# Stick-breaking attention in a decoder block: VectorE's weight copies one slot later, the gather matmuls two slots later, the y copies two slots later

## What is computed

```python
def block(args):
    logits = jnp.einsum('bqhd,bkhd->bhqk', qi, k) * scale
    mask = key_pos[None, :] < q_pos[:, None]
    log_beta = jax.nn.log_sigmoid(logits)
    log_1m_beta = jnp.where(mask, jax.nn.log_sigmoid(-logits), 0.0)
    after = lax.cumsum(log_1m_beta, axis=3, reverse=True) - log_1m_beta
    w = jnp.where(mask, jnp.exp(log_beta + after), 0.0)
    return jnp.einsum('bhqk,bkhd->bqhd', w, v)
```

## Time and profile before

| | |
|---|---|
| median of 3 runs | 2943.34 us (2942.4 to 2946.0) |
| profiled execution, its own time | 2947.28 us |
| its span in the profile | 2944.7 us |
| mean granted TensorE clock | 0.970 of full speed |
| PE busy | 2750.3 us (93% of the span) |
| DVE, ACT, POOL busy | 1854.0, 1373.1, 924.1 us |
| the attention stage | from about 600 to 1096 us in the span |

### The profile page before, as it was taken

How to read it: one execution, slowest core, us unless ns; L and a number is a source line. 1 busy time by engine, 2 the same in 40 slices (tenths; PEclk the granted TensorE clock), 3 DMA queues, 4 the chain that set the end, 5 groups by cost and what they waited for, 6 DMA issues and landing times. The chain is left out here.

```text
span 2944.7 us, 43748 instructions
## 1 busy us (share of the span) xinstructions
PE 2750.3 (93%) x14835; PEld 2242.1 (76%) x14835; DVE 1854.0 (63%) x2853; ACT 1373.1 (47%) x2508; POOL 924.1 (31%) x839
## 2 busy tenths in 40 slices
PE   6999977879999989996999899999999999999998
PEld 5888864757777767885888688887888787878787
DVE  5343338958878876555667765656556748484853
ACT  4222224668878774323444455555554424242421
POOL 0011100746666652120000032333233334444442
PEclk9999988989999999997999999999999999999999
DMA  5433345282322204423222344334534465647554
GB/s 172 107 80 91 88 130 71 61 216 67 74 62 55 80 21 150 137 86 136 94 86 105 107 136 133 103 100 155 170 129 131 129 157 100 168 104 171 98 114 86
DMA packets 291144, 328.23 MB, mean 111 GB/s; under 512 B 113816, under 2 KB 220320, under 8 KB 290720
## 3 DMA queue, kind: packets, MB, share of 16 engines
q1 hardware_dynamic: 276704, 291.96, 33.2%
q0 software_dynamic: 13824, 33.56, 7.7%
q10 hardware_dynamic: 464, 0.79, 0.1%
HBM read 206.57 MB, written 126.88 MB: 113 GB/s over the span
## 5 line engine op out<-in xcount | busy, mean ns | idle before, releaser
L3252 PE MATMUL f_ps_bank<-f_big,h_wv 128*128 128x512 f32 x1280 | 503.0, 393 | 24.4 <-DVE f_big L3098 17.5
L3253 PE MATMUL f_ps_bank<-f_big,h_wv 128*128 128x512 f32 x1280 | 500.8, 391 | 0.0
L3254 PE MATMUL f_ps_bank<-f_big,h_wv 128*128 128x512 f32 x1280 | 500.7, 391 | 0.0
L736 POOL TENSOR_TENSOR a_w<-a_on,a_left 128x512 f32<-128x512 f32 (+3 forms) x320 | 304.3, 955 | 183.5 <-DVE a_left L784 168.8
L2995 ACT ACTIVATE h_wv<-h_w_sum 128x512 fp32r<-128x512 f32 x252 | 158.9, 631 | 347.0 <-PE f_ps_bank L3254 316.7
L2938 POOL TENSOR_TENSOR h_w_sum<-h_w_raw 128x512 f32<-128x512 f32 x63 | 90.2, 1432 | 731.1 <-DMA h_w_raw<-in_w_up 453.8
L3252 PEld LDWEIGHTS f_ps_bank<-f_big,h_wv 128*128 128x128 f32 x1280 | 241.9, 189 | 81.7 <-issue 26.3
L3254 PEld LDWEIGHTS f_ps_bank<-f_big,h_wv 128*128 128x128 f32 x1280 | 241.8, 189 | 50.9
L3253 PEld LDWEIGHTS f_ps_bank<-f_big,h_wv 128*128 128x128 f32 x1280 | 241.7, 189 | 49.5
L3094 DVE TENSOR_TENSOR h_wv<-h_w_raw,h_wv 128x512 fp32r<-128x512 f32 x189 | 175.1, 927 | 158.3 <-ACT h_wv L2995 154.2
L749 ACT ACTIVATE a_on<-a_ps_z 128x512 f32<-128x512 f32 (+3 forms) x320 | 170.9, 534 | 94.1 <-PE a_ps_z L842 53.0
(11 more groups left out here) (401 smaller groups left out, 6129.2 us busy)
## 6 DMA issues: line engine op xcount, KB each, us to landing
h_w_raw<-in_w_up SPq DMA_DIRECT2D x32, 1024.0 KB, 6.7
a<-h_xr SPq DMA_DIRECT2D x128, 256.0 KB, 3.4
h_w_raw<-a SPq DMA_DIRECT2D x32, 1024.0 KB, 5.2
h_raw<-in_w_down SPq DMA_DIRECT2D x32, 512.0 KB, 6.6
out<-h_xr POOLq DMA_DIRECT2D x64, 256.0 KB, 4.7
out<-h_xr POOLq DMA_DIRECT2D x32, 512.0 KB, 5.6
p_xt<-in_x SPq DMA_DIRECT2D x16, 512.0 KB, 4.7
q<-p_raw SPq DMA_DIRECT2D x64, 128.0 KB, 2.5
```

The lines of the kernel that those rows point to most:

```text
L736: pool.tensor_tensor(w[m % WS][:, 0:k1 - k0], on[m % ONS][:, 0:k1 - k0], left[a][i % 2][:, at + k0 + 1:at + k1 + 1], ALU.mult).then_inc(we ...
L3252: pe.matmul(o, wv(i, 0)[:, k, :], hv(i, 0)[:, k, :], start=(k == 0), stop=False)
L3253: pe.matmul(o, wv(i, 0)[:, k, :], hv(i, 1)[:, k, :], start=False, stop=False)
L3254: mm = pe.matmul(o, wv(i, 1)[:, k, :], hv(i, 0)[:, k, :], start=False, stop=(k == KH - 1))
```

## The change

Three of the six lags are raised; nothing else is touched. No instruction is added or removed, no buffer changes its size or number.

```diff
     ZS, ONS, WS, WTS = 5, 6, 6, 8
-    LEAD, TURN_LAG, ACT_LAG, DVE_LAG, GATHER_LAG, Y_LAG = 4, 3, 7, 4, 5, 7
+    LEAD, TURN_LAG, ACT_LAG, DVE_LAG, GATHER_LAG, Y_LAG = 4, 3, 7, 5, 7, 9
```

## The result

| | before | changed |
|---|---|---|
| median | 2942.87 us (4 runs) | 2918.50 us (4 runs, 2913.3 to 2920.7) |
| ratio to before | | 0.9913, 95% interval 0.9896 to 0.9930 |
| profiled execution, span | 2947.28, 2944.7 us | 2917.92, 2915.0 us |
| first to last matmul of the attention | 482.7 us | 455.3 us |
| DVE waits for turns before weight copies | 64.3 us, 78 times | 23.6 us, 25 times |

The change makes the kernel faster by 24.4 us in the medians; the forecast was 15.7. The two profiled executions stand 29.4 us apart, of which 27.4 are in the attention.

The account below looks back on a forecast made before the run. PE was taken to set the pace, losing time where its score loads wait for DVE's scans. Waits -16, start -0.7, end +1.0 and boundaries 0 sum to -15.7 us from 2943.3: 2927.6 us, range 2919 to 2939.

Parts of the forecast that it names:

- the working's 2.0 us: In attention, DVE's weight copy, scan and handovers take about 2.0 us, against 1.94 us of PE work.
- the first term of the sum: Attention score loads waiting for DVE's scans: 16 us won, between 4.7 and 22.1.
- the prediction's boundaries: Three step boundaries, stretches of 12 us each such as 736 to 748, opening at slot 89's score.
- the one on the boundaries: Ten scan waits at the three step boundaries stay, 4.2 us; boundary change 0, between -1.5 and +1.5 us.
- the end: After the last turn, three pairs are gathered instead of two: +1.0 us, between 0 and 1.0.
- the start: Scan(6) comes before the copy that waits for slot 2's turn: -0.7 us, between 0 and -1.2.
- The half clock stays: At the step boundaries the lower clock remains after the change, within a boundary term of 0.
- What the later copy adds: PE's turn can now wait for DVE's copy behind a scan; cost taken as nothing, covered by DVE's lead.
- Rival C: DVE gains no lead, so turns wait 0.2 us at each of 106 copies: 2964 us, chance 0.06.
- Gather and y copy: Both move two slots later: nothing in the middle of a step, +1.0 us at the end.
- Rival A: Weight loads' waits were covered, so only what PE's row shows returns: 4.4 us, 2939 us, chance 0.09.
- Rival B: Another wait, for POOL, ACT or a slow DVE, replaces the scan's; some 3 us remain, 2940 us, chance 0.10.

Follow-up runs that it names:

- run one slot earlier: Kernel before with only DVE's weight copy one slot earlier (lags 3, 5, 7); 3105.8 us, ratio 1.0553.
- run with the old lags and the early store: Kernel before (lags 4, 5, 7) with SP storing y's third quarter before loading the next step's second half; 2931.8 us, ratio 0.9963.
- the early store: SP issues the store of y's third quarter before the loads of the next step's second half; on the changed kernel 2905.2 us, ratio 0.9877.
- the run with the y copy first on ScalarE: Lags 6 and 7, y copies moved from DVE to ScalarE, 12 iterations back, ahead of its sigmoids; 2909.1 us, ratio 0.9894 to the kernel before.

## Why the prediction was right and wrong

- **The mechanism** was right: DVE's wait for a turn put its scans behind, PE's scores waited for them, and one more iteration of distance removed it. The weight copy alone gives it. The run one slot earlier shows the working's 2.0 us of copy, scan and handovers.
- **The step that failed is the first term of the sum, the size of the scan waits: "I take nine tenths, 16 us".** The waits outside the prediction's boundaries gave 22.8 us (18.4 inside the steps and 4.4 just before the boundaries). Nine tenths took off 1.9 of the 17.9 us counted, though next to nothing stayed. The count itself was short by 4.9. The starts of the matmuls in the run with the old lags and the early store, whose boundaries have the full clock, put all scan waits at 18.4 + 7.4 = 25.8 us, where 22.1 had been called real. Two reasons can be seen. A score behind a gather that lost nothing has a gap of 0.17 us, not 0.19. And two waits behind a gather stand in the list under "issue", though the matmul's own row gives them to the scan, as here in the kernel before (the other is at 882.54, 0.48 us):

```profile
844.56 0.19 PEld L839 LDWEIGHTS a_ps_z<-a_k_hi,a_q 128*128 128x128 f32 x1 [0.79 <-issue]
844.59 0.30 PE L839 MATMUL a_ps_z<-a_k_hi,a_q 128*128 128x128 f32 x1 [0.57 <-DVE a_left L784]
```

  Together these are some 2 us; the rest of the shortfall is not accounted for wait by wait.
- **The second step that failed is the one on the boundaries**: "They come from short slots, where DVE is simply slower than PE, and stay", and with it "I take 0" for them. Of the 4.2 us kept back, 2.9 are found at the full clock, and all of them went. With the copy alone later, 1.4 of these 2.9 do stay; they go when gather and y copy come later too. DVE isn't slower than PE in short slots: with the early store PE waits 0.2 us for a scan in each boundary stretch. Between the two traces the boundaries proper gave 3.7 us in place of 0.
- **The sum of the miss**: 6.8 from the first term, 3.7 from the boundaries, 1.0 from the end and 0.1 from the start make, but for rounding, the 11.7 us between 15.7 forecast and 27.4 traced. In the medians the miss is 8.7.
- **The bounds**: "Its own bounds are 2943.3 - 22.1 - 1.2 = 2920" leaves out the -1.5 us that the text itself gives the boundaries; with them the low bound is 2918.5. The upper bound, "about 2936", does not follow from the terms either: 4.7 us for the waits, 0 at the start, +1.0 at the end and +1.5 at the boundaries make 2941.
- **"The half clock stays"** holds for the changed kernel (0.95, 0.95, 0.96 over the boundary stretches; 0.96, 0.92, 0.92 before). It goes with the store's wait in every run with the early store. That wait is needed for it, but not enough, as the run with the y copy first on ScalarE shows.
- **What the later copy adds** was put at nothing, and inside the steps it is nothing. At one boundary the turn waits 2.7 us for a copy that stands behind the y copy's wait for the store. Rival C is real, but one slot further off.
- **Gather and y copy**: "Nothing in the middle of a step" holds (317.0 against 318.0 us). +1.0 at the end is 0.9 to 1.2 in the runs that show it alone; in the whole change the end came out even (18.2 us in both), since the later copy alone shortens it by 0.9. That they do something at the boundaries with the early copy, 3 us in the median, I had not seen; why is not settled.
- **Rival A** fell: inside the steps alone, where the clock is full in both traces, the attention became 18.4 us shorter, where PE's row had promised 7.2 over the whole. The case in which the page's rule would have hidden the waits (the Trainium skill, TensorE: Matmul & The Clock Gate, section on the array as 16× 32×32) did not come about: in the run one slot earlier, PEld's row stands idle for 2.02 us before the waiting score, with no later weight load in it.
- **Rival B** fell: inside the steps no engine took the scan's place; 74.9 us is what every run needs there once the waits are gone.
- **The signs**: PEld's wait for scans fell under 15 us as said (6.9). DVE's wait for turns did not (23.6). The y store waits did not stay near 2 us each but grew from 6.9 to 8.7 in all. PE's busy row was to grow in share and not in time; it stayed at 93% and fell by 24.8 us (2750.3 to 2725.5), since that row had hidden the waits.

## What to carry to other kernels

When two engines wait for each other, count the distance in iterations between the producer of each wait and its consumer, and compare it with the work in between: here 1.94 us of PE against 2.0 us of DVE, short by a tenth of a microsecond at one scan and some three tenths at the next, cost about 25 us over 106 copies. An engine's early arrival is worth nothing if a later wait in its own order gives it back, so after a wait is moved, look at the next one in the same queue before moving it further. A transfer queue has such an order as well: a store that a coming step needs should not stand behind loads that wait for the running step's last work.

## What the runs showed of the hardware

A wait of a weight load in front of its matmul is lost time of PE almost one for one, less the 0.17 us that a load behind a gather idles in any case, though PE's busy row hides most of it, because matmuls count until their modelled end. In the run with the old lags and the early store, loads behind a turn waited 16.2 us for scans, and the starts of the matmuls lost 16.8.

An idle of PE amid short slots at a boundary may be followed by a stretch at the lower of the two clock levels. In the traces before and after the change each of the six idles, of 1.5 to 2.7 us, was (granted clock 0.92 to 0.96 over some 40 us). But with the y copy first on ScalarE three idles of 1.5 to 1.7 us were not, and in the run with the copy two slots later one of 2.5 us, at 980.55, was not. The length of the idle alone does not decide it; what does is open. Where the store came early there was no such idle, and the clock stayed at 1.00 over the boundaries.

In the profiled kernel before, the store's stall and that clock together cost 13.0 us in three places, where PE's waits for the y copy add up to 5.0.
